# Moving a strict causal mask from VectorE and GpSimd into TensorE products (one core, fp32 block)

## The chip, the cores and the metric

One Trainium2 chip, one core. The metric is device time in microseconds for one execution of the whole program. The kernel before takes 1555.07 us, the median of 3 runs (1554.88 to 1556.66).

## The reference

Two transformer blocks on 512 tokens of width 1024, all in fp32: the first has three attention branches (a sparse one with an index, a stick-breaking one with 8 heads of width 64, and one over a memory), a gated merge and a feed-forward part; the second an mLSTM layer and a dilated-window attention. The change touches the stick-breaking branch alone:

```python
def stick_breaking_attention(bq, bk, bv):        # 8 heads, QBLK = 128, HEAD_DIM = 64
    def block(i):
        z = jnp.einsum('bqhd,bkhd->bhqk', q_b, bk).astype(jnp.float32) * HEAD_DIM ** -0.5
        causal = kpos[None, :] < qpos[:, None]
        log_beta = jax.nn.log_sigmoid(z)
        log_one_minus = jnp.where(causal, jax.nn.log_sigmoid(-z), 0.0)
        tail = lax.cumsum(log_one_minus, axis=log_one_minus.ndim - 1, reverse=True) - log_one_minus
        a = jnp.where(causal, jnp.exp(log_beta + tail), 0.0).astype(bv.dtype)
        return jnp.einsum('bhqk,bkhd->bqhd', a, bv)
```

A query never sees itself or a later key (strictly causal). The weights are exp(z minus the sum of softplus(z) over this key and the keys between it and the query).

## The kernel before

Every engine has one hand-written program; they meet at semaphores. Big products run as three fp32r products of high and low halves (`mm3`, L729 to L733); every matrix product of TensorE goes through `mm` and so is recorded on L732 (transposes on L761). The weights of such products come in slabs: SyncE loads `raw`, ScalarE rounds it to `w_hi` (L1474), GpSimd takes the difference `w_lo` (L559, in quarters L579), TensorE uses both.

The stick-breaking part lies between the second `bv` slab and the gate slabs, from 284 to about 356 us. A head's scores are held transposed, keys on partitions, as four tiles (key tile kt against queries from 128 kt on: 512, 384, 256 and 128 columns), packed into 1280 columns of PSUM (`stick_at`, two places in turn) and of `stick_a[h % 4]`. FIRST is the tile of key tile 0 (512 columns), LATER the other three (768 columns). The first 128 columns of each tile are its diagonal square, the only one which needs a mask.

The loop over steps (TensorE L1101 to L1132, ScalarE L1697 to L1728, VectorE L2237 to L2265) is a software pipeline. In step s:

- TensorE makes the logits of head s (`stick_z_mm`, plain fp32, 64 rows, two records for each product), first tiles 1, 3, 2, then tile 0; each group waits until ScalarE has read the same PSUM of head s-2 (`st_a`) and then signals `st_z`. In steps 3, 5, 7 and 9 it makes the values of a pair of heads (`stick_pair`, L1079), after GpSimd has masked both (`st_am`). Then it adds, for head s-1, the sums over keys to the logits in place (`stick_sums`: constants `sums_r` times `sp_hi` and `sp_lo`, LATER and then FIRST) and signals `st_r`.
- ScalarE, for head s: abs (L1706) of LATER and FIRST, exp(-abs) (L1709) of both, then ln(1+..) (L1713) of LATER, the weights' exp (L1717) of LATER of head s-1, and the same two for FIRST.
- VectorE, for head s, each half: softplus = max(z, 0) + ln (L2243) into `sp_raw`, then products with the constant square `bmask` on the diagonal squares (L2247, L2249 for LATER, L2252 for FIRST), the rounded `sp_hi` (L2255) and the rest `sp_lo` (L2257).
- GpSimd, when both weight halves of a head are there (`st_a`): two selects that set the weights of the diagonal squares to zero where the key isn't below the query (`keep_causal`, L613 to L618), signal `st_am`; for heads 2 to 5 then a quarter of the gate slab's `w_lo`.

In step 8 the first gate logits are put between the last sums, behind a wait for `st_a`; `stick_pair(3)` comes behind the first gate slab. The constant squares `sq` are loaded at the start (L442, L498); VectorE casts two of them to fp32r as `sums_r` (L2236) ahead of the loop.

Of the kernel before, what the change touches and what calls it, by code (L numbers as in the profile page):

```python
# [113 lines left out]
V_GAIN = {n: 8 * i for i, n in enumerate(["x", "mem", "ffn", "a2", "kv3", "b3", "g0", "g1"])}  # L114
V_BGATE, V_CONV, V_HEAD, V_ROWS = 64, 88, 120, 128

SQ = {n: i for i, n in enumerate(["ident", "ntri", "nones", "bmask", "mmask", "adm"])}

TILE_AT = [0, 512, 1024, 896]
TILE_N = [512, 384, 256, 128]  # L120
# [4 lines left out]
def constants():  # L125

    p, f = np.arange(P)[:, None], np.arange(P)[None, :]
    sq = np.zeros((P, len(SQ), P), np.float32)
    sq[:, SQ["ident"]] = p == f
    sq[:, SQ["ntri"]] = -1.0 * (p >= f)  # L130
    sq[:, SQ["nones"]] = -1.0
    sq[:, SQ["bmask"]] = p < f
    sq[:, SQ["mmask"]] = np.where(p <= f, 0.0, NEG)
    sq[:, SQ["adm"]] = np.where((p < 64) & (f >= 64), FILL, 0.0)
    rel = (np.arange(SPAN) - 511).astype(np.int32)
    n = np.abs(rel)
    ratio = np.log(np.maximum(n, 1).astype(np.float32) / np.float32(8)) / np.float32(math.log(16)) * np.float32(8)
    large = np.minimum(8 + ratio.astype(np.float32).astype(np.int32), 15)
    bucket = np.where(rel > 0, 16, 0) + np.where(n < 8, n, large)
    onehot = (np.arange(BUCKETS)[:, None] == bucket[None, ::-1]).astype(np.float32)  # L140
    inv = np.float32(10000.0) ** (-np.arange(0, 128, 2, dtype=np.float32) / np.float32(128))
    ang = np.arange(S, dtype=np.float32)[:, None] * inv[None, :]
    rope = np.stack([np.cos(ang), np.sin(ang)], 1).astype(np.float32)

    q, k = p, np.arange(4 * P)[None, :] - 3 * P
    dil = np.zeros((P, 256 + 512 + 512), np.float32)
    dist = q - k
    dil[:, 0:256] = np.where((dist >= 0) & (dist <= 128), 0.0, NEG)[:, 256:]
    for i, r in ((0, 4), (1, 16)):
        dil[:, 256 + 512 * i:768 + 512 * i] = np.where((dist >= 0) & (dist % r == 0), 0.0, NEG)  # L150
    return {"c_sq": sq.reshape(P, -1), "c_onehot": onehot, "c_rope": rope, "c_dil": dil}
# [74 lines left out]
def _program(nc, A, ctx):  # L226
# [3 lines left out]
    def place(name, kib, words, dtype=F32, parts=P):  # L230
        return nc.alloc_sbuf_tensor_at(name, [parts, words], dtype, offset=SB0 + int(kib * 1024))

    def arena(name, kib, words, dtype=F32, parts=P):
        return place(name, ARENA + kib, words, dtype, parts)

    def sem(name):
        return ctx.enter_context(nc.semaphore(name))
# [41 lines left out]
    def const(name):  # L279
# [21 lines left out]
    stick_a = [arena(f"stick_a{n}", k, PACK) for n, k in enumerate((72, 82, 48, 53))]  # L301
    sp_raw, sp_hi, sp_lo = arena("sp_raw", 77, PACK), arena("sp_hi", 87, PACK, F32R), arena("sp_lo", 58, PACK, F32R)
    sums_r = place("sums_r", 103.5, 2 * P, F32R)
    aqkT = arena("aqkT", 32, 8 * S)
    ya_hi, ya_lo = arena("ya_hi", 32, 4 * S, F32R), arena("ya_lo", 40, 4 * S, F32R)
    av = arena("av", 58, NT * HALF)
# [76 lines left out]
    sums_made, st_sl = sem("sums_constants"), sem("stick_sp_lo")  # L383
    at_y = sem("attn_bank_read")
    mask_made, offset_made = sem("masks_made"), sem("offset_made")
    st_z, st_ln, st_sp, st_r, st_a, st_am, st_pv, st_hi, st_lo = (sem(n) for n in (
        "stick_z", "stick_ln", "stick_sp", "stick_r", "stick_a", "stick_masked", "stick_pv", "stick_hi", "stick_lo"))
    cv, cv_sig = sem("conv_done"), sem("conv_sig")
    merge_step, ffn_step = sem("merge_step"), sem("ffn_step")
    lo_merged, lo_ffn, cv_mul = sem("merged_lo_made"), sem("ffn_lo_made"), sem("conv_first_silu")  # L390
# [161 lines left out]
    def _(pool):  # L552
# [57 lines left out]
            second(3)  # L610
            root(pre, 2, 2)

        def keep_causal(buf, done, strict):  # L613

            for part in diagonals(buf):
                ins = pool.affine_select(out=part, in_=part, pattern=[[0, 2], [1, P]], compare_op=ALU.is_gt if strict else ALU.is_ge,
                                         fill=0.0, base=0, channel_multiplier=-1)
            ins.then_inc(done, 1)  # L618

# [27 lines left out]
            if 0 <= quarter < 4:  # L647
                lo_quarter(BASE["bqk"] + s + 1, quarter)
        split_lo(BASE["bv"] + 1, BASE["gate"] + 1)
        for h in range(8):  # L650
            pool.wait_ge(st_a, 2 * h + 2)
            keep_causal(stick_a[h % 4], st_am, True)
            if 2 <= h < 6:
                lo_quarter(BASE["gate"] + 1, h - 2)
        def ffn_piece(s):

            return lambda n: lo_quarter(BASE["ffn_in"] + s, (0, 2, 1, 3)[n], seam_lo)
# [22 lines left out]

        for h in range(4):
            pool.wait_ge(m_e, h + 1)
            keep_causal(decay[h % 2], m_em, False)
            if h >= 2:
                head_root(h - 2)
            for quarter in ((), (0, 1), (2,), (3,))[h]:
                lo_quarter(BASE["wout2"] + 1, quarter)
# [42 lines left out]
    def _(pe):  # L730
# [334 lines left out]
        def stick_z_mm(h, tiles):  # L1065
            rows = slice(64 * (h % 2), 64 * (h % 2) + 64)
            for kt in tiles:
                ins = mm(stick_tiles(h)[kt], bqkT[rows, (4 + h // 2) * S + kt * P:(4 + h // 2) * S + (kt + 1) * P],
                         bqkT[rows, (h // 2) * S + kt * P:(h // 2 + 1) * S], kt != 3, False, skip_group_check=True)
            ins.then_inc(st_z, 1)  # L1070

        def stick_sums(h, part, pairs):
# [5 lines left out]

        def stick_pair(p):  # L1079

            pe.wait_ge(st_am, 2 * p + 2)
            if p >= 2:
                pe.wait_ge(st_lo, p - 1)
            for kt in range(NT):
                for b in range(2):
                    h = 2 * p + b
                    ins = mm(banks[64 * b:64 * b + 64, p % 2, kt * P:], bv[:, kt * HALF + h * 64:kt * HALF + (h + 1) * 64],
                             stick_a[h % 4][:, TILE_AT[kt]:TILE_AT[kt] + TILE_N[kt]], kt == 0, kt == NT - 1, skip_group_check=True)
            ins.then_inc(st_pv, 1)

        def first_stick_z():

            pe.wait_ge(at_lo, 8)
            pe.wait_ge(ev_a, EV_A["bv"] + 1)
            pe.wait_ge(ev_v, EV_V["bv"] + 1)
            stick_z_mm(0, (1, 3, 2))
            stick_z_mm(0, (0,))
# [3 lines left out]
        for step in range(1, 8 + 2):  # L1101
            if step < 8:
                for n, tiles in enumerate(((1, 3, 2), (0,))):
                    if step >= 2:
                        pe.wait_ge(st_a, 2 * (step - 2) + n + 1)
                    stick_z_mm(step, tiles)
            if step == 3:
                pe.wait_ge(ev_a, EV_A["gate"])
                pe.wait_ge(ev_v, EV_V["gate"])
            if step >= 3 and step % 2 == 1:  # L1110
                stick_pair((step - 3) // 2)
            if step == 1:
                pe.wait_ge(sums_made, 1)
            if step == 8:
                pe.wait_ge(st_a, 14)
                gate_logits(wait_slab("gate", 0, 0, 0, 6), 0, 2)
            if step <= 8:
                h = step - 1
                later = [(jt, kt) for kt in range(1, NT) for jt in range(1, kt + 1)]
                pe.wait_ge(st_sp, 2 * h + 1)  # L1120
                stick_sums(h, sp_hi, later)
                pe.wait_ge(st_sl, 2 * h + 1)
                stick_sums(h, sp_lo, later).then_inc(st_r, 1)
                if step == 8:
                    gate_logits(BASE["gate"] % 2, 2, 3)
                first = [(0, kt) for kt in range(NT)]
                pe.wait_ge(st_sp, 2 * h + 2)
                stick_sums(h, sp_hi, first)
                pe.wait_ge(st_sl, 2 * h + 2)
                stick_sums(h, sp_lo, first).then_inc(st_r, 1)  # L1130
            if step == 8:
                gate_slab(0, 0, begun=3)  # L1132
# [875 lines left out]
    def _(dve):  # L2008
# [8 lines left out]
        def each_slab(stage, empty, first=0, count=None):  # L2017
            def body(i, s, j):
                g, slot, _ = at(BASE[stage], i, s)
                dve.wait_ge(slab_used, g + 1)  # L2020
                empty(i, s, j, slot)
            over_slabs(dve, stage, body, first, count)
# [210 lines left out]
            beside(BESIDE_A, step, empty_a)  # L2233

        each_slab("bv", to_rows(bv, HALF), 0, 1)
        dve.tensor_copy(sums_r[:], sq[:, SQ["ntri"] * P:(SQ["ntri"] + 2) * P]).then_inc(sums_made, 1)  # L2236
        for step in range(8 + 2):  # L2237
            for n, c in enumerate((LATER, FIRST)) if step < 8 else ():
                at_z = stick_at(step)
                dve.wait_ge(st_ln, 2 * step + n + 1)  # L2240
                if step:
                    dve.wait_ge(st_sl, 2 * step - 1 + n)
                link(dve.scalar_tensor_tensor(out=sp_raw[:, c], in0=flat[:, at_z + c.start:at_z + c.stop], scalar=0.0,  # L2243
                                              in1=stick_a[step % 4][:, c], op0=ALU.max, op1=ALU.add))
                if n == 0:
                    d = sp_raw[:, TILE_AT[1]:TILE_AT[1] + P]
                    dve.tensor_tensor(d, d, const("bmask"), ALU.mult)  # L2247
                    d = sp_raw[:, TILE_AT[3]:TILE_AT[3] + 2 * P].rearrange("p (t c) -> p t c", t=2)
                    link(dve.tensor_tensor(d, d, const("bmask").unsqueeze(1).broadcast_to([P, 2, P]), ALU.mult))  # L2249
                else:  # L2250
                    d = sp_raw[:, 0:P]
                    link(dve.tensor_tensor(d, d, const("bmask"), ALU.mult))  # L2252
                if step:
                    dve.wait_ge(st_r, 2 * step)
                dve.tensor_copy(sp_hi[:, c], sp_raw[:, c]).then_inc(st_sp, 1)  # L2255
# [367 lines left out]
```

## Time and profile before

| | |
|---|---|
| median of 3 runs | 1555.07 us |
| profiled execution, first to last instruction | 1553.7 us |
| TensorE busy | 1529.0 us (98%) |
| VectorE, ScalarE, GpSimd busy | 703.0, 601.9, 693.8 us |
| stick-breaking part | about 284 to 356 us |

The span is that of the profiled execution; it stands 1.4 us under the median of the runs. TensorE's granted clock is 1.000 throughout, which is its upper level (2.4 GHz). Records of products overlap, since a product's record lasts until its results are written; what a product takes in a dense stream is the distance from its start to the next start.

### The profile page before, as it was taken

How to read it: one execution, taken by the hardware profiler on the slowest of the kernel's cores; microseconds unless marked ns; L12 is line 12 of the kernel's file. 1: busy time of each engine (PE TensorE's matmuls, PEld its weight loads, DVE VectorE, ACT ScalarE, POOL GpSimd, SP SyncE). 2: the span in 40 equal slices, each digit the busy share in tenths (PEclk: the TensorE clock that was granted, in tenths of full speed). 3: DMA queues.
4: the chain of work that ended last, by engine and by line, in shares of the span. 5: the costliest groups of instructions: out<-in, count | busy, mean ns of one | idle time of the engine just before them, and what ended most of it. 6: DMA issues, size and time to landing. Idle time of an engine off the chain costs nothing.

```text
span 1553.7 us, 19713 instructions
## 1 busy us (share of the span) xinstructions
PE 1529.0 (98%) x7588; PEld 1253.4 (81%) x7588; DVE 703.0 (45%) x1147; ACT 601.9 (39%) x916; POOL 693.8 (45%) x312
## 2 busy tenths in 40 slices
PE   8999999999999999999999999999999999999898
PEld 7777967877888888888888888888888888887687
DVE  4258855482334226665654005630034346444733
ACT  6353254673332225122221115422444444355452
POOL 6423455334555535443434444444432435454532
PEclk9999999999999999999999999999999999999999
DMA  7314211102333332433332225543422322222021
GB/s 246 122 55 136 82 55 49 41 21 61 102 101 87 109 109 70 118 97 104 85 108 86 104 82 72 99 104 92 126 68 72 101 89 82 95 82 82 28 72 64
DMA packets 145126, 138.26 MB, mean 89 GB/s; under 512 B 7792, under 2 KB 118384, under 8 KB 145052
## 3 DMA queue, kind: packets, MB, share of 16 engines
q1 hardware_dynamic: 140836, 130.79, 29.3%
q10 hardware_dynamic: 4216, 6.45, 1.3%
q8 instruction: 51, 0.84, 0.2%
q14 instruction: 23, 0.19, 0.0%
HBM read 135.09 MB, written 2.13 MB: 88 GB/s over the span
## 4 chain that ended last, share of the span: by engine, by line
PE 90%; DVE 3%; ACT 3%; POOL 2%; issue 1%; DMA 0%; ACTq 0%; DVEq 0%; POOLq 0%
PE banks L732 87%; PE banks L761 2%; POOL w_lo L579 1%; PE banks L920 1%; PE banks L1350 0%; DVE prob L2552 0%; DVE xs L2072 0%; ACT w_hi L1474 0%; POOL prob L721 0%; DMA vec_rows<-in_norm_a 0%; ACT junk L1523 0%; ACT k L1938 0%; POOL prob L723 0%; ACT junk L1762 0%; DVE head_ms L2514 0%
## 5 line engine op out<-in xcount | busy, mean ns | idle before, releaser
L559 POOL TENSOR_TENSOR w_lo<-raw,w_hi 128x2048 fp32r<-128x2048 f32 x104 | 481.4, 4629 | 602.3 <-ACT w_hi L1474 602.3
L732 PE MATMUL banks<-h_hi,w_hi 128*128 128x512 f32 (+1 forms) x904 | 348.1, 385 | 2.4 <-DVE h_lo L2079 0.9
L732 PE MATMUL banks<-h_hi,w_lo 128*128 128x512 f32 (+1 forms) x904 | 340.4, 377 | 0.0
L732 PE MATMUL banks<-h_lo,w_hi 128*128 128x512 f32 (+1 forms) x904 | 340.1, 376 | 0.0
L1474 ACT ACTIVATE w_hi<-raw 128x2048 fp32r<-128x2048 f32 (+2 forms) x123 | 233.1, 1895 | 213.3 <-PE banks L732 203.1
L732 PEld LDWEIGHTS banks<-h_hi,w_hi 128*128 128x128 f32 x904 | 169.9, 188 | 42.1 <-issue 9.7
L732 PE MATMUL banks<-w_hi,h_hi 128*128 128x512 f32 (+1 forms) x544 | 199.8, 367 | 0.0
L732 PE MATMUL banks<-w_hi,h_lo 128*128 128x512 f32 (+1 forms) x544 | 198.2, 364 | 0.0
L732 PE MATMUL banks<-w_lo,h_hi 128*128 128x512 f32 (+1 forms) x544 | 198.1, 364 | 0.0
L732 PEld LDWEIGHTS banks<-h_hi,w_lo 128*128 128x128 f32 x904 | 169.6, 188 | 32.2
L732 PEld LDWEIGHTS banks<-h_lo,w_hi 128*128 128x128 f32 x904 | 169.9, 188 | 29.5
L579 POOL TENSOR_TENSOR w_lo<-raw,w_hi 128x512 fp32r<-128x512 f32 x84 | 113.6, 1373 | 104.3 <-ACT w_hi L1474 92.1
L732 PEld LDWEIGHTS banks<-w_hi,h_hi 128*128 128x128 f32 x544 | 102.6, 189 | 16.9 <-issue 1.1
L732 PEld LDWEIGHTS banks<-w_hi,h_lo 128*128 128x128 f32 x544 | 102.6, 189 | 16.2
L732 PEld LDWEIGHTS banks<-w_lo,h_hi 128*128 128x128 f32 x544 | 102.7, 189 | 15.8
L2351 DVE TENSOR_TENSOR f_lo<-ff_prod,f_hi 128x512 f32 x22 | 104.2, 4738 | 2.7
L1794 ACT ACTIVATE ff_sig<-banks 128x512 f32<-128x512 f32 x22 | 13.2, 600 | 175.9 <-PE banks L732 175.9
L732 PE MATMUL banks<-w_hi,f_lo 128*128 128x512 f32 x176 | 68.5, 389 | 0.0
L732 PE MATMUL banks<-w_hi,f_hi 128*128 128x512 f32 x176 | 68.5, 389 | 0.0
L732 PE MATMUL banks<-w_lo,f_hi 128*128 128x512 f32 x176 | 68.5, 389 | 0.0
L1735 ACT ACTIVATE gate<-banks,col 128x512 f32<-128x512 f32 x24 | 16.6, 690 | 130.5 <-PE banks L732 130.5
L2060 DVE TENSOR_REDUCE meansq<-sumsq 128x1 f32<-128x2 f32 (+4 forms) x19 | 2.9, 153 | 139.3 <-ACT junk L1762 130.4
(319 smaller groups left out, 2348.6 us busy)
## 6 DMA issues: line engine op xcount, KB each, us to landing
raw<-in_w_in SPq DMA_DIRECT2D x56, 512.0 KB, 4.0
raw<-in_w_ffn_in SPq DMA_DIRECT2D x44, 512.0 KB, 5.0
raw<-in_w_in_a SPq DMA_DIRECT2D x32, 512.0 KB, 5.7
raw<-in_w_ffn_out SPq DMA_DIRECT2D x22, 512.0 KB, 4.0
raw<-in_w_ple_gate SPq DMA_DIRECT2D x16, 512.0 KB, 4.6
raw<-in_w_in_b SPq DMA_DIRECT2D x16, 512.0 KB, 4.5
raw<-in_w_out SPq DMA_DIRECT2D x8, 512.0 KB, 4.0
raw<-in_w_out_a SPq DMA_DIRECT2D x8, 512.0 KB, 4.5
```

Of the source, the lines that this page charges most:

```text
L559: pool.tensor_tensor(slot_of(w_lo, slot), slot_of(raw, slot), slot_of(w_hi, slot).bitcast(F32), ALU.subtract).then_inc(lo_made, 1)
L579: ins = pool.tensor_tensor(w_lo[:, c], raw[:, c], w_hi[:, c].bitcast(F32), ALU.subtract)
L732: return pe.matmul(out, lhsT, rhs, start=start, stop=stop, **kw)
L761: ins = pe.transpose(banks[:, transposed_bank(name, k), t * P:(t + 1) * P], rows(t)[:, k * P:(k + 1) * P], const("ident"))
L920: ins = pe.transpose(banks[:, 6, kt * P:(kt + 1) * P], src[:, kt * P:(kt + 1) * P], const("ident"))
L1474: act.activation(slot_of(w_hi, slot, words), slot_of(raw, slot, words), ACT.Copy).then_inc(hi_made, 1)
L1735: act.activation(gate[slot][:], banks[:, 2 * slot, :], ACT.Sigmoid, bias=col[:, ds(V_BGATE + KD * (s % 3) + ft, 1)]).then_inc(ev_a, 1)
L1794: act.activation(ff_sig[:], banks[:, 2 * slot, :], ACT.Sigmoid).then_inc(ev_a, 1)
L2060: link(dve.tensor_reduce(meansq[:, c], pieces, AX_X, ALU.add))
L2351: dve.tensor_tensor(lo, ff_prod[:], hi.bitcast(F32), ALU.subtract).then_inc(lo_ffn, 1)
```

## The change

The constants `bmask` and `mmask` go, `below` comes: 0 where the key is below the query, -2^100 elsewhere. VectorE casts the identity and `below` to fp32r (`below_r`) ahead of `sums_r`. Behind the logits of each group TensorE adds, for each tile, the product of the identity with `below` to its diagonal square (128 columns), in the same accumulation; `st_z` is signalled behind these. Masked logits are then -2^100: their softplus is 0 and their weight exp gives 0, so VectorE's mask products and GpSimd's selects go, and `stick_pair` waits for ScalarE's `st_a` directly. The wait for `sums_made` moves from step 1 to ahead of the first logits. GpSimd's quarter slabs keep their wait for `st_a`.

```diff
-SQ = {n: i for i, n in enumerate(["ident", "ntri", "nones", "bmask", "mmask", "adm"])}
+SQ = {n: i for i, n in enumerate(["ident", "ntri", "nones", "below", "adm"])}
...
-    sq[:, SQ["bmask"]] = p < f
-    sq[:, SQ["mmask"]] = np.where(p <= f, 0.0, NEG)
+    sq[:, SQ["below"]] = np.where(p < f, 0.0, -2.0 ** 100)
...
+    below_r = arena("below_r", 63, 2 * P, F32R)
...
-        for h in range(8):
+        for h in range(2, 6):
             pool.wait_ge(st_a, 2 * h + 2)
-            keep_causal(stick_a[h % 4], st_am, True)
-            if 2 <= h < 6:
-                lo_quarter(BASE["gate"] + 1, h - 2)
+            lo_quarter(BASE["gate"] + 1, h - 2)
...
             for kt in tiles:
                 ins = mm(stick_tiles(h)[kt], bqkT[rows, (4 + h // 2) * S + kt * P:(4 + h // 2) * S + (kt + 1) * P],
                          bqkT[rows, (h // 2) * S + kt * P:(h // 2 + 1) * S], kt != 3, False, skip_group_check=True)
+            for kt in tiles:
+                ins = mm(stick_tiles(h)[kt][:, 0:P], below_r[:, 0:P], below_r[:, P:2 * P], False, False, skip_group_check=True)
             ins.then_inc(st_z, 1)
...
         def stick_pair(p):
 
-            pe.wait_ge(st_am, 2 * p + 2)
+            pe.wait_ge(st_a, 4 * p + 4)
...
             pe.wait_ge(at_lo, 8)
+            pe.wait_ge(sums_made, 1)
...
-            if step == 1:
-                pe.wait_ge(sums_made, 1)
...
+        dve.tensor_copy(below_r[:, 0:P], const("ident"))
+        dve.tensor_copy(below_r[:, P:2 * P], const("below"))
         dve.tensor_copy(sums_r[:], sq[:, SQ["ntri"] * P:(SQ["ntri"] + 2) * P]).then_inc(sums_made, 1)
...
-                if n == 0:
-                    d = sp_raw[:, TILE_AT[1]:TILE_AT[1] + P]
-                    dve.tensor_tensor(d, d, const("bmask"), ALU.mult)
-                    d = sp_raw[:, TILE_AT[3]:TILE_AT[3] + 2 * P].rearrange("p (t c) -> p t c", t=2)
-                    link(dve.tensor_tensor(d, d, const("bmask").unsqueeze(1).broadcast_to([P, 2, P]), ALU.mult))
-                else:
-                    d = sp_raw[:, 0:P]
-                    link(dve.tensor_tensor(d, d, const("bmask"), ALU.mult))
```

## Rows read from the trace of the kernel before

**Rows 1.** The page: span, and busy time of TensorE.
```profile
span 1553.7 us, 19713 instructions
PE 1529.0 (98%) x7588; PEld 1253.4 (81%) x7588; DVE 703.0 (45%) x1147; ACT 601.9 (39%) x916; POOL 693.8 (45%) x312
```
**Rows 2.** TensorE's waits, whole run: for whom, us in total, times, longest us.
```profile
PE banks L732 <- ACT stick_a L1717: 1.4, 3, 0.7
...
PE banks L732 <- POOL stick_a L616: 0.6, 1, 0.6
...
PE banks L732 <- DVE sp_hi L2255: 0.4, 2, 0.2
PE banks L732 <- DMA sq<-in_c_sq: 0.4, 1, 0.4
```
**Rows 3.** Busy time by stretch, steps 4 and 5; first the stretch, its length, TensorE.
```profile
315.20:321.00 5.80, 5.58 (x30) 4.15 (x29) 5.48 (x8) 5.33 (x10) 2.84 (x3) 1.00 0.00 0
321.00:328.57 7.57, 7.57 (x45) 5.07 (x44) 6.80 (x12) 5.50 (x9) 3.15 (x3) 1.00 0.00 0
```
**Rows 4.** Timeline of TensorE, merged, step 5: start, us, what.
```profile
323.35 2.37 PE L732 MATMUL banks<-stick_a,bv 128*64 128x512 f32 x16
325.66 0.96 PE L732 MATMUL banks<-sp_hi,sums_r 128*128 128x384 f32 x6
```
**Rows 5.** The chain that ended last, in order of time: start, us, what.
```profile
297.88 0.60 ACT stick_a L1706
...
308.03 1.82 POOL stick_a L616 x2
...
317.57 1.41 DVE sp_raw L2252
```
**Rows 6.** Timeline of ScalarE, step 4, single records.
```profile
317.67 0.60 ACT L1706 ACTIVATE stick_a<-banks 128x512 f32<-128x512 f32 x1
318.16 0.83 ACT L1709 ACTIVATE stick_a<-stick_a 128x768 f32<-128x768 f32 x1
...
320.15 0.80 ACT L1717 ACTIVATE stick_a<-banks 128x768 f32<-128x768 f32 x1
```
**Rows 7.** Groups by line and form, 284 to 355 us: busy us, mean ns, idle before.
```profile
L2252 DVE TENSOR_TENSOR sp_raw<-sp_raw,sq 128x128 f32<-128x128 f32 x8 | 5.3, 659 | 0.3
...
L616 POOL TENSOR_SCALAR_AFFINE_SELECT stick_a<-stick_a 128x256 f32<-128x256 f32 x16 | 11.5, 741 | 42.8 <-ACT stick_a L1717 42.8
```
**Rows 8.** Timeline of TensorE, step 4, single records: tile 0's logits, the sums' ends.
```profile
316.61 0.59 PE L732 MATMUL banks<-bqkT 64*128 64x512 f32 x1
317.04 0.59 PE L732 MATMUL banks<-bqkT 64*128 64x512 f32 x1
317.56 0.44 PE L732 MATMUL banks<-sp_hi,sums_r 128*128 128x384 f32 x1
...
318.25 0.27 PE L732 MATMUL banks<-sp_hi,sums_r 128*128 128x128 f32 x1
318.36 0.39 PE L732 MATMUL banks<-sp_lo,sums_r 128*128 128x384 f32 x1
...
320.84 0.22 PE L732 MATMUL banks<-sp_lo,sums_r 128*128 128x128 f32 x1
```
**Rows 9.** Timeline of TensorE, single records where head 0's logits begin and end.
```profile
284.03 0.28 PE L732 MATMUL banks<-w_hi,h_lo 128*128 128x256 f32 x1
284.24 0.59 PE L732 MATMUL banks<-bqkT 64*128 64x384 f32 x1
284.67 0.48 PE L732 MATMUL banks<-bqkT 64*128 64x384 f32 x1
...
286.60 0.39 PE L732 MATMUL banks<-w_hi,h_hi 128*128 128x256 f32 x1
286.82 0.28 PE L732 MATMUL banks<-w_lo,h_hi 128*128 128x256 f32 x1
286.94 0.29 PE L732 MATMUL banks<-w_hi,h_lo 128*128 128x256 f32 x1
```

More of the change, by code:

```diff
@@ L385, in _program @@
     mask_made, offset_made = sem("masks_made"), sem("offset_made")
-    st_z, st_ln, st_sp, st_r, st_a, st_am, st_pv, st_hi, st_lo = (sem(n) for n in (
-        "stick_z", "stick_ln", "stick_sp", "stick_r", "stick_a", "stick_masked", "stick_pv", "stick_hi", "stick_lo"))
+    st_z, st_ln, st_sp, st_r, st_a, st_pv, st_hi, st_lo = (sem(n) for n in (
+        "stick_z", "stick_ln", "stick_sp", "stick_r", "stick_a", "stick_pv", "stick_hi", "stick_lo"))
     cv, cv_sig = sem("conv_done"), sem("conv_sig")
@@ L611, in roots_and_pieces, with keep_causal @@
             root(pre, 2, 2)
-        def keep_causal(buf, done, strict):
+        def keep_causal(buf, done):
             for part in diagonals(buf):
-                ins = pool.affine_select(out=part, in_=part, pattern=[[0, 2], [1, P]], compare_op=ALU.is_gt if strict else ALU.is_ge,
+                ins = pool.affine_select(out=part, in_=part, pattern=[[0, 2], [1, P]], compare_op=ALU.is_ge,
                                          fill=0.0, base=0, channel_multiplier=-1)
@@ L682, in _ @@
             pool.wait_ge(m_e, h + 1)
-            keep_causal(decay[h % 2], m_em, False)
+            keep_causal(decay[h % 2], m_em)
             if h >= 2:
```

## The prediction

> **What bounds the kernel now.** I start with the page: TensorE is busy in 98% of the span [rows 1]. Only where TensorE waits, or where its own work grows or shrinks, can the end move. The second view is the list of TensorE's waits: in this stage it waits 1.4 us for ScalarE's exponential (L1717), 0.6 us for GpSimd's mask (L616) and 0.4 us for VectorE's `sp_hi` [rows 2], 2.4 us in all. That is all that a faster mask on the other engines can remove directly, of 1555 us.
>
> The third view is the stage cut into the steps of its loop. A step with a value product (`stick_pair`, steps 3, 5, 7) is dense on TensorE: step 5 takes 7.57 us with 7.57 us busy. A step without one (steps 1, 2, 4, 6) takes 5.80 us with 5.58 us busy [rows 3], though its work fits in less: the value products take 325.66 - 323.35 = 2.31 us [rows 4], so 7.57 - 2.31 = 5.26 us is what such a step needs. So 5.80 us is a loop, and the question is which.
>
> The chain of waits names two candidates: in steps 1 and 2 it runs from the logits to ScalarE's absolute value (L1706), in steps 4 and 6 through VectorE's mask, a 128x128 product of 1.41 us (L2252) [rows 5]. The chain shows only one of two paths that end nearly together, so I check with ScalarE's own timeline in step 4 [rows 6]: the logits start at 315.20, the second absolute value (tile 0, which waits for `st_z` of the last logits) starts 2.47 us later, the two exponentials at 318.16, and the exponential for the weights at 320.15 with 0.80 us to run, which ends at 320.95; the next logits start at 321.00. They wait for exactly that (`st_a` of head h-2). So the loop of a 5.80 us step is logits (all tiles), then ScalarE's abs, exp, ln and exp, then the next logits. VectorE's mask is not in it.
>
> **What goes.** On VectorE three mask products a head, the longest 0.66 us on average (L2252), drawn out to 1.41 us beside GpSimd's work [rows 5, 7]. Nearly all lies beside TensorE and ScalarE; what shows is the 0.4 us wait of TensorE in steps 4 and 6, and since the ScalarE loop sets these steps, I give back nothing for it. On GpSimd 16 selects of 0.74 us [rows 7]; what shows is the wait before the first `stick_pair`, 0.6 us [rows 2]. Pairs 1 to 3 never wait for GpSimd (one wait in the list), so these give nothing. With the select gone, `stick_pair(0)` waits for the exponential, 308.03 at the latest (where the select starts [rows 5]), and TensorE's logits of step 3 run to 307.01 + 2.36 = 309.37 anyway: the whole 0.6 us goes. The remaining quarter splits on GpSimd start about 1.5 us earlier and can meet another VectorE instruction, which has slack of the removed 1.4 us; zero. The constant table loses one of six squares; TensorE waits 0.4 us for it near 20 us [rows 2], so 0 to -0.4 us; I take 0.
>
> **What comes.** Four 128-column products a head on TensorE, 32 in all, fp32r with 128 rows, three between the logits of tiles 1, 3, 2 and those of tile 0, one behind tile 0. I need the pitch (start to start) of such a product and the price of going from the 64-row fp32 logits to 128-row fp32r and back, since the change puts one more such round trip into each head.
>
> Pitch: in the tail sums the last 128-column product starts at 318.25, the next instruction at 318.36: 0.11 us [rows 8]. Most of it is weight load (a 256-column product takes 0.12 as well [rows 9], and its columns are twice as many).
>
> Out of fp32: the last record of tile 0's logits takes 317.56 - 317.04 = 0.52, the one before 0.43 [rows 8]: +0.09. The first fp32r product behind takes 286.82 - 286.60 = 0.22 against 0.12 for the next [rows 9]: +0.10. Into fp32: the last fp32r product takes 284.24 - 284.03 = 0.21 against 0.12: +0.09, or 321.00 - 320.84 = 0.16 against 0.11 behind the sums [rows 8], +0.05. The first fp32 record, of 384 columns, takes 284.67 - 284.24 = 0.43 [rows 9], which a 512-column one takes in mid-stream (317.04 - 316.61 [rows 8]); 3/4 of that is 0.32: +0.11. A round trip is about 0.35 to 0.39 us.
>
> The Trainium skill ("TensorEngine Tiling (Array Packing)", Key Properties) says that changing the tiling mode drains TensorE. It speaks against this change, since the logits are 64-row tiles and the mask product has 128 rows; the trace's 0.09 to 0.11 us a piece agree. The Trainium skill also gives about 81 ns as the sustained pitch of 128-column products ("TensorE: Matmul & The Clock Gate", Back-to-back issue gap); by it the sum would be 32 x 0.03 = 1 us less, but the trace's 0.11 is used.
>
> From the start t of a head's logits then: tiles 1, 3, 2 take 316.61 - 315.20 = 1.41; +0.09 out of fp32; three mask products, the first with its 0.10, 0.21 + 0.115 + 0.115; +0.05 into fp32; tile 0's first record 0.43 + 0.11; second 0.43 + 0.09: 3.04 us. The last mask product takes 0.21 and the sums behind it lose their own first-product excess of 0.11. TensorE's part grows from 2.36 (317.56 - 315.20) to 3.04 + 0.21 - 0.11 = 3.14, by **0.8 us**. For ScalarE the last mask product must be finished, not only started: a 128-column record lasts some 0.3 us there, so abs of tile 0 starts at 3.04 + 0.3 + 0.04 = 3.38 instead of 2.47, by **0.9 us** later.
>
> **The sum.** Step 0 stands in the dense `bv` slab: +0.8. Steps 1, 2, 4, 6 are the ScalarE loop, abs of tile 0 is on it and waits for TensorE already: 4 x 0.9 = +3.6. (TensorE alone would need 5.26 + 0.8 = 6.06, under 5.80 + 0.9 = 6.7, so the loop still sets it.) Step 3: +0.8 - 0.6 = +0.2. Steps 5 and 7: 2 x 0.8 = +1.6. The 0.7 us wait ahead of the gate logits in step 8 is a ScalarE chain hanging on step 7's sums; it moves along unchanged. Step 8 has no logits. Together +6.2 us. The `below_r` casts on VectorE (two more before `sums_made`, which TensorE now waits for ahead of the first logits) cost 0.6 us at 282 where the logits start at 284.24: nothing. Behind the stage TensorE is dense, so the delay arrives at the end in full. Span 1553.7 + 6.2 = 1559.9; the median of the runs stands 1.4 us over the profiled span, so 1555.1 + 6.2 = **1561.3 us**.
>
> Bounds: a product costs at least its columns, half of the 0.12 us of a 256-column one, 0.06, and at most its full record without overlap, 0.27 [rows 8]. The round trip lies between 0 and 0.39. With pitch 0.11 and no trip price a head gets 0.46 us dearer: 8 x 0.46 - 0.6 = +3.1. With 0.27 and 0.36, 1.44: +10.9.
>
> **Rivals.**
> Cheap switches, +3.1 us (1558.2), 13%: the excesses I read are those of long products behind short ones and a 128-column product hides in them. For: the excess of 0.10 is a weight load that could cover 0.05 us of streaming. Against: it appears at every change of form in the trace.
> Dear products, +9.6 to +10.9 (1564.7 to 1566.0), 15%: the short product runs at the fp32 logits' rate (128 columns take two records of 0.11, so +0.11 x 32 = 3.4 on top of 6.2), or each waits for its own weights. For: nothing in the trace has the identity as weights between two fp32 groups. Against: the 128-column sums at 0.11.
> Not slower, +0.2 us (1555.3), 12%: the mask products cost their columns only, 32 x 0.06 = +1.9 us, and VectorE's mask, not ScalarE, is what holds steps 4 and 6 as the chain says, so that their lost time, 2 x 0.54 (5.80 - 5.26), goes with GpSimd's 0.6: -1.7, together +0.2. It decides if a head's logits grow by less than 0.2 us. Against it stands the 0.05 us between ScalarE's end and the next logits. A sixth of this case I give to a real gain, faster by over 0.2%.
> That the change doesn't do its work is no rival of time: large negative logits give exp 0 at the same price.
>
> **Chances.** Forecast 60% (own range 1560 to 1563), the rivals as said. A measurement of this kernel tells 0.2%, 3.1 us, from no change. Slower by more: 60 + 15 + half of cheap switches (7) = 82%. Within: 6 + 10 = 16%. Faster: 2%. The range 1557.8 to 1565.5 leaves out "not slower" and half of "dear products".
>
> **What would show it.** Right: steps 1, 2, 4, 6 of some 6.7 us with no wait for VectorE; steps 5, 7 of 8.4; 128-column mask products with a pitch of 0.11; abs of tile 0 some 3.4 us behind the first logits; no GpSimd wait ahead of `stick_pair(0)`. Wrong: logits of a head growing by much less or more than 0.8 us, or a step of 5.80 us that stays so: then ScalarE was not the loop.

## The result and the profile after

The changed kernel takes 1563.31 us (median of 5 runs, 1562.29 to 1566.32) against 1555.33 us for the kernel before: a ratio of 1.0049, 95% interval 1.0038 to 1.0060. It is 8.0 us slower; 6.2 were forecast, in a range of 1557.8 to 1565.5.

The page of the changed kernel, span and busy times:

```profile
span 1564.5 us, 19743 instructions
...
PE 1537.6 (98%) x7620; PEld 1258.3 (80%) x7620; DVE 692.7 (44%) x1125; ACT 601.9 (38%) x916; POOL 683.9 (44%) x296
```

VectorE and GpSimd have each lost some 10 us of work, TensorE has 8.6 us more, and TensorE is the engine that bounds ([rows 1] is the row of before). Part of the 8.6 us is a lower clock, shown below: in a second profiled run of the same kernel, without a fall of the clock, TensorE is busy 1534.5 us, 5.5 more than before. TensorE's waits, whole run (for whom, us in total, times, longest):

```profile
PE banks L730 <- ACT stick_a L1716: 3.1, 5, 0.7
...
PE banks L730 <- DMA sq<-in_c_sq: 1.8, 1, 1.8
```

Against [rows 2] the waits for GpSimd's mask and VectorE's `sp_hi` are gone, and the wait for ScalarE has grown from 1.4 to 3.1 us, five waits where there were three: the loop over ScalarE has become longer than TensorE's own work by 0.6 us in each of four steps. Steps 3 to 5 by stretch (its length, then TensorE, weight loads, VectorE, ScalarE, GpSimd, and behind them the granted clock), and a piece of step 5:

```profile
312.20:320.69 8.49, 8.49 (x49) 5.58 (x49) 4.43 (x7) 7.14 (x10) 0.00 (x0) 1.00 0.01 2
320.69:327.41 6.72, 6.11 (x34) 4.44 (x32) 4.90 (x7) 5.33 (x10) 2.08 (x1) 1.00 0.00 0
327.41:337.55 10.14, 10.14 (x48) 6.03 (x48) 4.79 (x7) 5.50 (x9) 1.93 (x1) 0.83 0.00 0
...
331.00:333.70 2.70, 2.70 (x8) 0.71 (x8) 0.64 (x2) 2.40 (x4) 0.00 (x0) 0.50 0.00 0
```

Step 4 has grown from 5.80 to 6.72 us [rows 3], with 0.6 us in which TensorE is idle. Step 5 shows something that the profile of before has nowhere in this stage: for at least 2.7 us the granted clock was 0.50, the lower level of 1.2 GHz, and the step took 10.14 us instead of the 8.49 of step 3. TensorE had waited 0.6 us for ScalarE at 305.5, at 312.2 and again at 327.4, some 3 us before the clock fell. The same run has a second fall, which has nothing to do with this stage: from 26.8 to 30.2 us, behind the wait of 1.8 us for the constants `sq`.

```profile
27.00:30.00 3.00, 3.00 (x16) 3.00 (x15) 1.50 (x4) 1.48 (x4) 1.97 (x2) 0.50 0.31 60
```

Records of TensorE in step 4 (start, us), the counterpart of [rows 8]; the row with x2 holds the second and the third mask product together. The ends of TensorE's records are modelled by the profile, so the starts are what is read:

```profile
320.69 0.59 PE L730 MATMUL banks<-bqkT 64*128 64x384 f32 x1
...
322.18 0.33 PE L730 MATMUL banks<-below_r 128*128 128x128 f32 x1
322.34 0.39 PE L730 MATMUL banks<-below_r 128*128 128x128 f32 x2
322.45 0.28 PE L730 MATMUL banks<-below_r 128*128 128x128 f32 x1
322.66 0.69 PE L730 MATMUL banks<-bqkT 64*128 64x512 f32 x1
323.19 0.59 PE L730 MATMUL banks<-bqkT 64*128 64x512 f32 x1
323.71 0.33 PE L730 MATMUL banks<-below_r 128*128 128x128 f32 x1
323.88 0.39 PE L730 MATMUL banks<-sp_hi,sums_r 128*128 128x384 f32 x1
```

The three mask products follow at 0.16 and 0.11 us, but 0.21 us pass from the third to tile 0's logits, whose first record takes 0.53 where it took 0.43. From the first logits to the sums it is 3.19 us; before, 2.36. And ScalarE in the same step, against [rows 6]:

```profile
324.08 0.60 ACT L1705 ACTIVATE stick_a<-banks 128x512 f32<-128x512 f32 x1 [0.44 <-PE banks L730]
324.57 1.35 ACT L1708 ACTIVATE stick_a<-stick_a 128x768 f32<-128x768 f32 x2
...
326.56 0.80 ACT L1716 ACTIVATE stick_a<-banks 128x768 f32<-128x768 f32 x1
```

The absolute value of tile 0 starts 324.08 - 320.69 = 3.39 us behind the first logits (before: 2.47; forecast: 3.38), and the four instructions behind it take as long as they did.

### The profile page after: what moved, and what is told of

Same layout as the page of the kernel before. It is cut to its first block, busy times and chain, and to the rows that moved or that the text cites. A ratio compares the mean times of both kernels' runs of the same rounds, so it can differ in the third digit from the quotient of the medians.

```text
span 1564.5 us, 19743 instructions
## 1 busy us (share of the span) xinstructions
PE 1537.6 (98%) x7620; PEld 1258.3 (80%) x7620; DVE 692.7 (44%) x1125; ACT 601.9 (38%) x916; POOL 683.9 (44%) x296
## 4 chain that ended last, share of the span: by engine, by line
PE 90%; ACT 3%; DVE 2%; POOL 2%; DMA 1%; issue 1%; ACTq 0%; SPq 0%; DVEq 0%; POOLq 0%
PE banks L730 87%; PE banks L759 2%; POOL w_lo L579 1%; PE banks L918 1%; DMA sq<-in_c_sq 1%; PE banks L1349 0%; DVE prob L2545 0%; ACT w_hi L1473 0%; POOL prob L719 0%; DMA vec_rows<-in_norm_a 0%; ACT stick_a L1708 0%; ACT k L1937 0%; ACT stick_a L1716 0%; POOL prob L721 0%; ACT junk L1761 0%
```

## The experiments

The kernels below were timed in three groups, each beside the kernel before on the same chip, which stood at medians of 1555.9 to 1556.1 us there. A step is the stretch from one head's first logits to the next one's; "the stage" is from the first logits of head 0 to the value products of the last pair: 353.86 - 284.24 = 69.62 us in the kernel before.

### The changed kernel once more

> The changed kernel once more, beside these three. Theory: lowest run +6.7 us over before's lowest, most runs 0.5 to 8 us above it, where the granted clock fell in the stage; steps 1, 2, 4, 6 of 6.72 us where it did not.

1563.56 us (1562.32 to 1571.74), ratio 1.0064 (1.0046 to 1.0082). In its profiled run the clock did not fall; by stretch:

```profile
297.08:303.81 6.73, 6.13 (x34) 4.45 (x33) 1.41 (x2) 4.74 (x8) 0.00 (x0) 1.00 0.00 0
303.81:310.54 6.73, 6.12 (x33) 4.45 (x33) 4.20 (x7) 5.10 (x9) 0.00 (x0) 1.00 0.00 0
310.54:319.04 8.50, 8.50 (x49) 5.58 (x49) 4.43 (x7) 7.13 (x10) 0.00 (x0) 1.00 0.01 2
319.04:325.76 6.72, 6.11 (x34) 4.44 (x32) 4.91 (x7) 5.33 (x10) 2.08 (x1) 1.00 0.00 0
325.76:334.25 8.49, 8.49 (x48) 5.58 (x49) 4.79 (x7) 5.50 (x9) 1.93 (x1) 1.00 0.00 0
```

The stage takes 361.40 - 285.12 = 76.28 us, 6.66 more than before, and what lies behind it takes 1199.8 us in both kernels. This is the cost of the change at full clock. The runs say nearly the same: of eleven runs of the changed kernel six had a mean granted clock of 1.000 and took 1562.3 to 1563.3 us. The middle one of the three beside this experiment stands 6.8 us over before's 1555.9, the middle one of the three beside the first comparison 7.2 over before's 1555.3. The five runs with 0.993 to 0.998 took 1564.1 to 1571.7.

A run's time also depends on when the stage begins, which varies from run to run: in the 14 profiles it begins anywhere between 284.2 and 287.2 us, and what lies behind it takes 1199.7 to 1199.9 us. So the lengths of the stage and its steps are compared below, and differences of a microsecond between medians are not all the stage's.

### The products alone

```diff
+            for kt in tiles:
+                ins = mm(stick_tiles(h)[kt][:, 0:P], below_r[:, 0:P], below_r[:, P:2 * P], False, False, skip_group_check=True)
             ins.then_inc(st_z, 1)
```

> The kernel before with the 32 mask products added and nothing taken away (VectorE's mask products, GpSimd's selects and their wait stay; the constant table keeps six squares, below in the place of the unused mmask). Theory (the products and their mode switches are the whole cost, and lengthen the ScalarE loop of steps 1, 2, 4, 6): +6.5 us over before, 1 us either way; steps 1, 2, 4, 6 of 6.72 us, step 5 of 8.4 to 8.5. GpSimd's wait ahead of the first value product goes as well, since the longer logits of step 3 cover it. Rival (what was taken off VectorE and GpSimd is worth something, so the products cost more than the change shows): +8 us or more, steps 1, 2, 4, 6 over 7.0 us with TensorE waiting for VectorE.

1565.18 us (1562.78 to 1571.26), ratio 1.0057 (1.0043 to 1.0071); the runs with clock 1.000 took 1562.8 and 1563.6 us. By stretch, the steps 2, 3 and 4 and a piece:

```profile
303.25:311.80 8.55, 8.55 (x32) 6.80 (x33) 6.05 (x12) 5.66 (x9) 1.81 (x2) 0.68 0.00 0
311.80:325.70 13.90, 13.90 (x50) 7.99 (x49) 5.11 (x9) 6.95 (x9) 1.58 (x2) 0.59 0.00 1
325.70:332.42 6.72, 6.13 (x34) 4.45 (x32) 5.93 (x8) 5.33 (x10) 2.83 (x3) 1.00 0.00 0
310.00:320.00 10.00, 10.00 (x26) 5.45 (x26) 4.51 (x9) 6.09 (x9) 1.58 (x2) 0.50 0.01 2
```

At full clock step 4 takes the same 6.72 us as in the changed kernel, and step 5 the same 8.50. With the products in place, the removal of all mask work on the other two engines saves nothing that these runs can tell. The median is 9.0 us over before, outside what was expected: four of the six runs had a mean clock of 0.998 or less. In the profiled one the clock stood at its lower level through most of steps 2 and 3, which cost (8.55 - 6.73) + (13.90 - 8.50) = 7.2 us by itself, and again from 350.6 to 354.0 us.

### Each removal alone

VectorE's mask products left out (the sums then contain unmasked diagonals):

> The kernel before without VectorE's three mask products a head and without anything in their place; it leaves out the mask in the sums, so the values are others. Theory (steps 1, 2, 4, 6 are a loop over ScalarE, VectorE is beside it): 0.0 us, steps 4 and 6 stay at 5.80 us although TensorE's 0.2 us waits for VectorE are gone. Rival (the chain of waits is right and VectorE's mask holds steps 4 and 6): -1.1 us, steps 4 and 6 of 5.3 us.

1557.04 us, ratio 1.0002 (0.9993 to 1.0011). Steps 3 to 6:

```profile
307.25:315.07 7.82, 7.64 (x45) 5.27 (x45) 4.43 (x7) 7.10 (x10) 1.43 (x2) 1.00 0.01 2
315.07:320.87 5.80, 5.53 (x31) 4.15 (x29) 5.52 (x7) 5.33 (x10) 2.84 (x3) 1.00 0.00 0
320.87:328.64 7.77, 7.64 (x45) 5.07 (x45) 5.57 (x7) 5.50 (x9) 2.72 (x3) 1.00 0.00 0
328.64:334.44 5.80, 5.53 (x31) 4.15 (x29) 5.52 (x7) 5.33 (x10) 2.83 (x3) 1.00 0.00 0
```

Steps 4 and 6 stay at 5.80 us, although the chain of waits ran through this very instruction (L2252 [rows 5]). What changed is whom TensorE waits for. Its last sums of step 4 and the logits behind them in the kernel before, and these logits in this one:

```profile
319.48 0.84 PE L732 MATMUL banks<-sp_hi,sums_r 128*128 128x512 f32 x4 [0.22 <-DVE sp_hi L2255]
321.00 2.42 PE L732 MATMUL banks<-bqkT 64*128 64x384 f32 x8
```
```profile
320.87 2.42 PE L732 MATMUL banks<-bqkT 64*128 64x384 f32 x8 [0.27 <-ACT stick_a L1717]
```

In the kernel before TensorE waits for VectorE, and the logits then follow the last sum without a wait. With the mask gone it waits for ScalarE instead, and the step is as long. The other steps do move, against each other: step 3 is 0.37 us shorter, since the selects ahead of its value products take 1.43 us instead of 1.81, and step 5 is 0.20 us longer, since its own take 1.47 instead of 1.20. The stage takes 354.17 - 284.48 = 69.69 us.

GpSimd's selects left out (the weights unmasked):

> The kernel before without GpSimd's selects; the value products wait for ScalarE's weights directly; it leaves out the mask on the weights. Theory: -0.6 us, all of it in step 3 (8.19 to 7.6 us), the other steps unchanged. Rival (the earlier quarter slabs on GpSimd disturb VectorE or ScalarE): 0 or slower, with steps 4 and 6 over 5.80 us.

1555.72 us, ratio 0.9995 (0.9987 to 1.0004), too close to tell from no change, but the steps tell it:

```profile
307.31:314.90 7.59, 7.59 (x45) 5.09 (x45) 5.97 (x12) 7.11 (x10) 0.00 (x0) 1.00 0.01 2
314.90:320.69 5.79, 5.32 (x30) 4.00 (x28) 5.21 (x8) 5.32 (x10) 2.08 (x1) 1.00 0.00 0
```

Step 3 falls from 8.19 to 7.59 us and no other step changes its length: the stage takes 353.56 - 284.54 = 69.02, 0.60 less. In steps 4 and 6 the wait for VectorE is gone here too, and TensorE waits 0.47 us for ScalarE. So ScalarE alone is enough to keep them at 5.80 us.

### What a product costs and what a switch costs

The mask products made twice in a row, each group:

```diff
+            for kt in tiles:
+                ins = mm(stick_tiles(h)[kt][:, 0:P], below_r[:, 0:P], below_r[:, P:2 * P], False, False, skip_group_check=True)
```

> The changed kernel (table of six squares) with every group of mask products made twice in a row: 32 more products, no more mode switches. Theory (pitch 0.115 us, and each lengthens TensorE's step and the ScalarE loop alike): +3.7 us over the changed kernel, some +10.3 over before; steps 1, 2, 4, 6 of 7.18 us, step 5 of 8.95. From it the split of a head's 0.83 us: 4 x 0.115 products and 0.37 switching. Rival (a product costs its 128 columns, 0.06 us, or its whole record, 0.27): +1.9 or +8.6 us over the changed kernel.

1568.75 us (1566.05 to 1571.85), ratio 1.0088 (1.0073 to 1.0104). Step 4:

```profile
320.27:327.45 7.18, 6.56 (x39) 4.90 (x37) 4.92 (x7) 5.34 (x10) 2.08 (x1) 1.00 0.00 0
```

The stage took 364.45 - 284.59 = 79.86 us at full clock, 3.58 more than in the changed kernel: 3.58 / 32 = 0.112 us a product. Of the 0.83 us that a head's logits grew by, 4 x 0.112 = 0.45 are products and 0.38 are switches. The switch from logits to mask products changes the number of rows and the data type at once. In the kernel before, the fp32 value products follow the last logits record after 0.52 us too (322.83 to 323.35), as the fp32r sums do (317.04 to 317.56), so that piece doesn't need the change of type; for the others no run here separates the two.

The mask products of tiles 1, 3, 2 ahead of their logits, so that no extra switch is needed (the mask product then begins the accumulation):

```diff
+            if 0 not in tiles:
+                for kt in tiles:
+                    mm(stick_tiles(h)[kt][:, 0:P], below_r[:, 0:P], below_r[:, P:2 * P], kt != 3, False, skip_group_check=True)
             for kt in tiles:
...
-            for kt in tiles:
-                ins = mm(stick_tiles(h)[kt][:, 0:P], below_r[:, 0:P], below_r[:, P:2 * P], False, False, skip_group_check=True)
+            if 0 in tiles:
+                ins = mm(stick_tiles(h)[0][:, 0:P], below_r[:, 0:P], below_r[:, P:2 * P], False, False, skip_group_check=True)
```

> The changed kernel (table of six squares), but the three mask products of tiles 1, 3, 2 stand ahead of their logits, behind the fp32r sums of the step before, and begin the accumulation; that of tile 0 stays behind its logits, ahead of the fp32r sums. So no head makes the extra round trip between fp32 and fp32r. Theory: TensorE's part grows by 0.40 us a head instead of 0.83, ScalarE's second abs comes 0.6 later than before instead of 0.9: +3.4 us over before, steps 1, 2, 4, 6 of 6.4 us, step 5 of 8.0. Rival (the switches are free and only the products cost): no gain over the changed kernel, +6.6.

1561.65 us (1559.69 to 1563.49), ratio 1.0035 (1.0021 to 1.0049). Steps 4 and 5:

```profile
319.19:325.72 6.53, 5.92 (x34) 4.52 (x33) 5.20 (x8) 5.48 (x10) 2.08 (x1) 1.00 0.00 0
325.72:333.88 8.16, 8.16 (x50) 5.60 (x49) 4.50 (x7) 5.36 (x9) 1.92 (x1) 1.00 0.00 0
```

The dense step falls from 8.49 to 8.16 us, which is a round trip of 0.33; the ScalarE-bound one only from 6.72 to 6.53, since the products now stand between the wait for ScalarE and the logits. The stage is 360.16 - 286.40 = 73.76 us, 4.1 over before where 3.4 were expected, and the three mask products of head 0 come on top: they start at 286.02, ahead of its first logits. The median is 1.6 us further up still. In the profiled run, which took as long as the median, that is the late start: the stage begins 2.2 us later than in the profile of before, behind a wait of 2.7 us for the constants instead of 0.4. TensorE's waits for ScalarE are the same four of 0.6 us as in the changed kernel, but all five runs have a mean clock of 0.999 or 1.000.

### Is ScalarE the loop?

In steps 1, 2, 4, 6 the exponential for which the next logits wait is put ahead of ln (`ln_of` and `weights_of` hold the lines that stood there, with their waits):

```diff
             for n, c in enumerate((LATER, FIRST)):
+                if step in (1, 2, 4, 6) and n == 0:
+                    weights_of(n, c)
+                    ln_of(n, c)
+                else:
+                    if step < 8:
+                        ln_of(n, c)
+                    if 1 <= step <= 8:
+                        weights_of(n, c)
```

In the changed kernel:

> The changed kernel (table of six squares); in steps 1, 2, 4, 6 ScalarE makes the weights' exp of the head before (LATER, for which the next logits wait) ahead of ln of this head instead of behind it. Theory (the ScalarE loop sets these steps): they fall from 6.72 us to what TensorE needs, about 6.05, and the time by 2.7 us, to +4.0 over before. Rival (TensorE's own products set them): no change.

1560.01 us (1559.04 to 1560.49), ratio 1.0025 (1.0015 to 1.0034). Step 4:

```profile
316.95:322.99 6.04, 6.04 (x34) 4.44 (x32) 4.19 (x6) 4.65 (x9) 2.08 (x1) 1.00 0.00 0
```

6.72 to 6.04 us, all of it busy: ScalarE was the loop, and what is left is TensorE's own work. The stage is 357.97 - 284.38 = 73.59, 2.7 less than the changed kernel at full clock. The ten runs lie within 1.5 us, and none has a mean clock under 0.999.

In the kernel before:

> The kernel before; in steps 1, 2, 4, 6 ScalarE makes the weights' exp of the head before (LATER) ahead of ln of this head. Theory (the loop over ScalarE sets these steps, VectorE's mask does not): steps 1, 4 and 6 fall from 5.80 us toward TensorE's 5.26, say 5.4, step 2 stays near 5.8 since its sums then wait for VectorE, which starts later: -1.0 to -1.6 us, so a kernel faster than both. Rival (the chain of waits is right, steps 4 and 6 end with VectorE's mask, which now starts 0.7 us later): +1 us or more.

1555.73 us (1554.89 to 1560.53), ratio 1.0001 (0.9992 to 1.0010): a miss. Steps 1, 2 and 4, and TensorE's waits (us in total, times, longest):

```profile
298.33:303.59 5.26, 5.26 (x30) 4.01 (x29) 0.69 (x1) 4.21 (x7) 0.00 (x0) 1.00 0.00 0
303.59:310.54 6.95, 6.08 (x30) 4.14 (x29) 5.72 (x10) 6.04 (x10) 1.04 (x2) 1.00 0.00 0
318.11:323.91 5.80, 5.58 (x31) 4.15 (x29) 5.26 (x8) 5.33 (x10) 2.84 (x3) 1.00 0.00 0
```
```profile
PE banks L732 <- DVE sp_hi L2265: 1.4, 4, 0.4
PE banks L732 <- ACT stick_a L1717: 0.7, 1, 0.7
```

Step 1 falls to exactly the 5.26 us which the prediction gave as TensorE's own need. Step 2 pays it back and more, since its sums wait for a VectorE that now starts later. Step 3 is 0.62 us shorter, since its value products no longer wait for GpSimd. Step 4 stays at 5.80 with a 0.2 us wait for VectorE. So in the kernel before two paths end together in steps 4 and 6, ScalarE's and VectorE's mask, and taking either one away gains nothing. The kernel before with both taken away, no mask on VectorE and the exponential first, was not run. The run of 1558.5 us is the profiled one: its stage takes 356.88 - 287.15 = 69.73 us, as before's, but begins 2.9 us later, behind a wait of 2.0 us for the constants and a granted clock of 0.50 from 27.2 to 30.6 us.

Both repairs of the changed kernel together:

> The changed kernel (table of six squares) with both repairs: the mask products of tiles 1, 3, 2 ahead of their logits, and the weights' exp ahead of ln in steps 1, 2, 4, 6. Theory: steps 1, 2, 4, 6 are TensorE's own work, 5.26 + 0.4 to 0.5 = 5.7 us, no wait left in them; over before 4 x -0.1 + 3 x 0.4 + 0.4 - 0.6 = +0.6 us, and the spread of the runs as small as before's. Rival (the extra work of the products can't be had back by order): +3 us or more.

1557.20 us (1556.65 to 1557.54), ratio 1.0008 (0.9999 to 1.0017). Steps 4 and 5:

```profile
316.32:322.12 5.80, 5.80 (x33) 4.52 (x32) 4.04 (x6) 4.75 (x8) 2.08 (x1) 1.00 0.00 0
322.12:330.28 8.16, 8.16 (x49) 5.57 (x48) 6.17 (x8) 6.09 (x11) 1.63 (x1) 1.00 0.00 0
```

Of the 7.7 us between the changed kernel and the one before in these runs 6.4 are had back. Step 4 is as long as before, but dense: 5.26 + 0.54, of which 4 x 0.112 = 0.45 are mask products. The stage is 355.85 - 284.99 = 70.86 us, 1.2 over before, and here too head 0's first mask products stand ahead of it, from 284.61. It doesn't beat the kernel before; it shows that the room the two waits left can hold the products, and no more.

### The clock

One more absolute value on ScalarE in steps 1, 2, 4, 6 of the kernel before, nothing on TensorE:

```diff
+                    if n and step in (1, 2, 4, 6):
+                        act.wait_ge(chain_a, chained(act.activation(e[:, c], z[:, c], ACT.Abs)))
                     made.append(chained(act.activation(e[:, c], z[:, c], ACT.Abs)))
```

> The kernel before with one more absolute value of tile 0 on ScalarE in steps 1, 2, 4, 6 (the same result written twice, with its end waited for), no work added on TensorE. It lengthens the ScalarE loop by about 0.65 us, as the mask products did (0.92), so TensorE stands idle more than 1 us in each of these steps. Theory of the clock (short waits of TensorE in this stage are what the fall of its granted clock follows, which the profiled runs of the changed kernel and of products_only show at 331 and at 306 us): median +2.6 us or more, some runs 2 to 8 us above their lowest, clock under 0.999 in these, and a lower granted clock in the stage of a profiled one. Rival (the fall comes of the small products or the switches, not of waiting): +2.6 us, all runs within 2 us.

1560.95 us (1560.05 to 1566.93), ratio 1.0038 (1.0025 to 1.0051). Steps 2, 4 and 5 and a piece of step 2:

```profile
302.93:311.36 8.43, 8.43 (x29) 6.30 (x29) 6.07 (x12) 6.16 (x10) 1.81 (x2) 0.60 0.00 0
319.07:325.50 6.43, 5.65 (x31) 4.15 (x29) 5.96 (x8) 5.93 (x11) 2.84 (x3) 1.00 0.00 0
325.50:335.27 9.77, 9.30 (x44) 5.54 (x45) 6.70 (x12) 5.50 (x9) 3.06 (x3) 0.83 0.00 0
...
306.00:311.00 5.00, 5.00 (x20) 4.75 (x20) 3.07 (x7) 4.39 (x7) 0.00 (x0) 0.50 0.00 0
```

At full clock a step takes 6.43 us, 0.63 longer, 2.5 us for four. The value products of steps 5 and 7 now wait 0.47 us each for GpSimd's select, which they don't in the kernel before. The clock fell twice: at 304.4, behind a wait of 1.1 us, and at 328.3, behind a wait of 0.6 us and with the one for the select. The median is 5.0 us up; the four runs with a mean clock of 0.999 are 4.2 to 5.3 up, the two with 0.996 and 0.995 7.4 and 11.0. There is not one mask product in this kernel, so neither the small products nor the switches are needed for a fall.

That the waits bring it is likely, but not shown. The kernels with a run under 0.999 and a fall in the profile of this stage all have waits of 0.6 us or more in steps 1 to 6, and those without such waits have no fall there. But the same waits don't always bring one: the changed kernel's second profiled run and the one with the products doubled had them and no fall, and the one with the mask first had them and neither a fall nor a run under 0.999. What decides between these is open.

### The constants

The unused square `mmask` left out of the kernel before, and an unused square put back into the changed kernel:

```diff
-SQ = {n: i for i, n in enumerate(["ident", "ntri", "nones", "bmask", "mmask", "adm"])}
+SQ = {n: i for i, n in enumerate(["ident", "ntri", "nones", "bmask", "adm"])}
```

> The kernel before with the unused square mmask left out of the constant table, nothing else. Theory A (the size of the load decides when it lands): TensorE's wait for the constants at 25 us grows from 0.4 to about 1.8 us and the time by 1.4 to 2.5 us. Theory B (it varies from run to run): within 0.7 us of before, the wait anything from 0.4 to 2 us.

> The changed kernel with one unused square put back into the constant table, so that its load has the size it has before. In the profile of the changed kernel TensorE waited 1.8 us for that load (0.4 before), at 26 us, and the stage began 2.5 us later. Theory A (the smaller load lands later by itself): the wait is 0.4 us again, the stage begins at 284.2 to 284.6 us, and the time is +6.6 us over before. Theory B (the landing varies from run to run): the time is within 1 us of the changed kernel's +8.0 and the wait may be anything from 0.4 to 2 us. Steps 1, 2, 4, 6 of 6.72 us and step 5 of 8.5 us in either, 8.5 and not the 10.1 us of the profiled run of the changed kernel, where the granted clock fell for some 3 us.

The first took 1556.13 us, ratio 1.0003 (0.9994 to 1.0012); the second 1565.87 us (1561.73 to 1571.67), ratio 1.0064 (1.0045 to 1.0083), its profiled run with the clock down in steps 5 and 7. Its step 5 took 10.09 us where 8.5 were expected, and its time is 9.7 us over before. Steps 1, 2, 4 and 6 take the same 6.73 us as in the changed kernel, so the size of the table doesn't lengthen them. TensorE's product behind the constants, with its wait, in the changed kernel, in the one with a square less, and in the one with a square more:

```profile
26.40 0.78 PE L730 MATMUL banks<-root_diag,sq 128*128 128x256 f32 x2 [1.85 <-DMA sq<-in_c_sq]
```
```profile
26.00 0.67 PE L731 MATMUL banks<-root_diag,sq 128*128 128x256 f32 x2 [1.43 <-DMA sq<-in_c_sq]
```
```profile
26.54 0.67 PE L730 MATMUL banks<-root_diag,sq 128*128 128x256 f32 x2 [1.35 <-DMA sq<-in_c_sq]
```

Over the 14 profiles of this case this wait lies anywhere between 0.2 and 2.7 us, with either size of table: 0.2 in the kernel with both repairs, 2.7 in the one with the mask first, both with six squares. The load's landing varies from run to run, and the 0.4 us in the profile of before was a short one.

## Why the prediction was right, point by point

- **What bounds the kernel.** Right in what decided the sum, incomplete beside it. "VectorE's mask is not in it" is refuted for steps 4 and 6 of the kernel before: VectorE's path ends with ScalarE's, as the reordered kernel showed. "They wait for exactly that" was read off two times that lie 0.05 us apart; the logits at 321.00 have no wait in the trace, they follow the last sum of 320.84 [rows 8], and TensorE's wait in that step was for VectorE. It cost the sum nothing, since the change removed one of the two paths and lengthened the other.
- **What goes.** 0 for VectorE: measured 0 (ratio 1.0002, steps 4 and 6 unchanged, the stage 0.07 us longer). 0.6 us for GpSimd: measured 0.60, in step 3. The earlier quarter slabs do meet another VectorE instruction: the 512-column rounding of `sp_hi` took 0.78 us beside them instead of 0.43, without effect on any step. The Trainium skill ("GPSIMD Engine Reference", 1. Specifications) lists the SBUF interfaces of GpSimd as shared with VectorE, with contention when the VectorE instruction is in a two-port mode or has two SBUF inputs. The two durations fit a shared interface; that the rounding, which has one input, runs in a two-port mode is not shown by any run.
- **What comes.** A product's pitch was put at 0.11, measured 0.112. A round trip was put at 0.35 to 0.39, measured 0.38 as the rest of a head's growth, 0.33 where it was taken out of a dense step. TensorE's part of a head: 0.8 forecast, 0.83 measured. ScalarE's second absolute value: 3.38 forecast, 3.39 measured.
- **The sum.** Step 0: 0.8 forecast, 11.96 - 11.18 = 0.78 measured. Steps 1, 2, 4, 6: 4 x 0.9 = 3.6 forecast, 0.93 + 0.94 + 0.92 + 0.93 = 3.72 measured. Step 3: 0.2 against 8.50 - 8.19 = 0.31. Steps 5 and 7: 1.6 against 0.92 + 0.91 = 1.83. Together 6.2 against 6.66 at full clock. The term which was mis-sized is that of steps 3, 5 and 7: behind the last mask product stand fp32 value products there, not fp32r sums, so the switch is paid once more and the "first-product excess of 0.11" which I let the sums lose is not lost. Three times 0.11 are most of the difference.
- **What was missing.** The fall of the clock. The forecast put nothing on what the longer idle time of TensorE in steps 1, 2, 4, 6 could bring. Some runs fall to 1.2 GHz for 3 us or more: one such fall made step 5 1.65 us longer. The median of all runs stands 0.7 us over the middle one of the undisturbed runs in the first comparison (1563.31 against 1562.57) and 0.9 in the second, and the runs up to 1571.7 all have a lower mean clock. No rival held it either. A mean doesn't say where the clock fell: in the first profiled run one of two falls lay ahead of the stage.
- **What that leaves.** The forecast of 6.2 us stands against 6.66 for the stage at full clock. The 8.0 us of the comparison hold 0.7 of the clock and some 0.6 more between the undisturbed runs (7.2) and the stage (6.66). For this the runs offer only the start of the stage, which varies by up to 2.9 us from profile to profile; it is not shown. The median 1563.31 lies in the stated range, but 0.3 us outside the narrower 1560 to 1563 that was given for the forecast itself.
- **The rivals.** "Cheap switches" fell with 0.38 us a head in them. "Dear products" fell with 0.112 us a product. "Not slower" fell twice: the logits grew by 0.83 us, and without VectorE's mask the steps stayed.

## What to carry to other kernels

Work taken off engines that have slack is worth only the waits which the bounding engine had for it, here 0.6 us. Work put on the bounding engine counts in full where that engine is dense, and if it stands ahead of a signal it lengthens the loop behind that signal as well; only where the engine waits, and the order can be changed so that it doesn't, does the wait hold the new work. A small product costs what it stands between: four of them cost 0.45 us, and changing the form of product in the middle of a group another 0.38, which placing them beside products of their own form takes out again. Where the chain of waits names one path, look for a second that ends with it before paying to remove the first.

## What the runs showed of the hardware that was not expected

- Four waits of TensorE of about 0.6 us each, one a step, can be followed by a fall of the granted clock to 0.50, its level of 1.2 GHz, for 3.4 us and more. Runs with a mean clock under 0.999: five of eleven of the changed kernel, four of six with the sixth square, four of six with the products alone, two of four with the products doubled, but none of five with the mask first, which has the same waits. With the same products and without the waits (the exponential first: ten runs within 1.5 us; both repairs: eleven within 0.9) neither a profile nor a run showed it, and with longer waits and without the products a profile did. The profile of the kernel before, in whose stage TensorE waits 2.4 us in six pieces, most of them 0.5 us or less [rows 2], and those of its variants without VectorE's mask, without the selects and with five squares, show none in this stage.
- Going once from 64-row fp32 products to 128-row fp32r ones and back costs 0.33 to 0.38 us. Two of the pieces are in the records of the changed kernel: 0.21 us from the last mask product to the logits instead of 0.11, and 0.53 for the first logits record instead of 0.43.
- The granted clock also fell to 0.50 near the start of the program, for 3.4 us, behind a wait for the constants of 1.8 us in the changed kernel's first profile and of 2.0 us in that of the kernel before with the exponential first. It did not behind the 2.7 us wait of the kernel with the mask first.
- VectorE and GpSimd held each other up whole instructions long. VectorE's 128x128 mask product takes 0.29 us alone. In step 4 of the kernel before it starts at 317.57, 0.04 us behind GpSimd's difference (317.53, 1.29 us long), and ends at 318.97, 0.15 us behind that one's end. In the changed kernel VectorE's `sp_lo` starts first, at 321.46, and takes its usual 0.96 us; GpSimd's difference starts 0.01 us behind it and takes 2.08 us instead of 1.29. VectorE's softplus of 512 columns, which reads PSUM, took 0.68 us beside GpSimd's work and without it.
- A small constant load that is queued among weight loads lands between 0.2 and 2.7 us after TensorE wants it, run by run.
